# Expert weights fetched in longer pieces: gate and up chunks of 2 k-blocks x 1024 columns, down chunks with two neighbouring rows in each partition

## The chip, the cores and the metric

One of the eight cores of a Trainium2 chip runs the whole program. The metric is the device time of one execution in microseconds. Before the change it is 1585.43 us, the median of 3 runs (1585.12 to 1586.38).

## What is computed

The reference is two stacks of two layers each on 256 tokens of width 1024, all in float32. Only the last layer's feed-forward part, a mixture of eight experts, is touched by the change (hidden width 3584, two experts for each token):

```python
def swiglu(h, wg, wu, wd):
    return (jax.nn.silu(h @ wg) * (h @ wu)) @ wd

def moe_swiglu(h, w_router, wg, wu, wd):
    ...
    logits = (xt @ w_router).astype(jnp.float32)
    top_v, top_i = lax.top_k(logits, TOP_K)
    gates = jax.nn.softmax(top_v, axis=-1)
    gate = jnp.sum(jax.nn.one_hot(top_i, N_EXPERTS, dtype=jnp.float32) * gates[..., None], axis=1)
    y = jnp.zeros_like(xt)
    for e in range(N_EXPERTS):
        y = y + gate[:, e:e + 1].astype(xt.dtype) * swiglu(xt, wg[e], wu[e], wd[e])
```

Before it come a mixer layer pair (attention, convolution, gating), a second mixer with pooling and dilated attention, a dense swiglu of hidden width 2816 and a second such mixer; after it a final rmsnorm. Each expert's three matrices are 1024 x 3584, 1024 x 3584 and 3584 x 1024 floats.

## The kernel before

**Chunks.** Every large weight goes through one ring. SP (`sync_program`, for the experts `sp_chunk_moe`, L708 to L714) issues a DMA of one 1 MiB chunk into one of `RAW = 6` buffers `raw`, once DVE has finished with the chunk that lay there (`lo_ready`). ACT copies the chunk to `whi`, rounded to the shorter type fp32r (`act_hi_moe`, L993, two instructions of 128x1024, `hi_ready`). DVE subtracts that from the raw chunk and writes the rest to `wlo` (`dve_lo_moe`, L1374, two of 128x1024, `lo_ready`). `whi` and `wlo` have `SPLIT = 3` buffers; PE frees one when it has used it (`split_used`), so ACT starts the rounding of step i + 3 when PE ends step i.

**Jobs.** The experts' tokens are gathered into jobs: a heavy job takes 128 rows of one expert, a light job 64 rows. A pair is one heavy and one light job, and here four pairs cover the eight experts. A job is 42 chunks: 28 for gate and up and 14 for down, a pair 84 steps, all pairs 336. For each 128-row block of weights a heavy step multiplies three times (low part of x by high weights, high by low, high by high: L2595 to L2597), twelve matmuls of 512 columns in all; in a light step high and low part of x lie side by side in the 128 rows, so it multiplies twice (L2610, L2611), eight matmuls, and the two halves of the rows are added later by `fold`.

**Gate and up.** `job_chunks` cuts a job's hidden width into `BLOCKS = 7` blocks p of 512 columns. A block has two gate chunks and then two up chunks, each 4 k-blocks x 512 columns (`KC = 4`, `NC = 512`). Gate is summed in PSUM bank 0 of the job's two (`acc[:, job, 0]`), up in bank 1. After the last gate chunk of a heavy block ACT writes silu of the bank to `act_h` (L1294), after the last up chunk DVE multiplies bank 1 into it (L2046), two steps later PE transposes it (L2694, 4 matmuls), ACT rounds the result to `ahi2` (L1298) and DVE takes the rest to `alo2` (L2055). For a light block ACT copies the gate bank to `gate_l` (L1305) and the up bank to `value_l` (L1317), PE folds each (L2648, 8 matmuls), ACT applies silu (L1311), DVE multiplies (L2061), and ACT and DVE split the product into `alT` (L1321, L2066).

**Down.** The 28 row blocks of 128 hidden rows come as 14 chunks of 2 row blocks x 1024 columns; the row block k is rows 128k to 128k + 127, row 128k + p in partition p. Both banks of the job gather the 1024 output columns. They are read (`y_read`, L1278; `y_lo`, L2036) and scattered back into x (L2570, L2571, and `scattered`, L2025).

**Order.** `FIRST_ORDER` and `PAIR_ORDER` list which job each of a pair's 84 steps serves. The first pair leads with 12 heavy chunks (`LEAD = 12`), since the light job's expert is known only then; five of its chunks (steps 6 to 10) are loaded ahead into tiles that are still empty (`AHEAD`). From then on heavy and light alternate, and so they do in the other pairs, but for the first and last few steps. `plan_of` puts the silu, transpose, fold and split of a block a fixed number of steps behind its last chunk. Within one step i each engine has a fixed order: ACT first rounds chunk i + 3 (for which it waits until PE has ended step i) and then does silus and copies of step i; DVE first multiplies a heavy block that ended with step i, and then splits chunk i + 3. PE waits in `heavy_waits` and `light_waits` before the first chunk of a block, until the bank it is going to fill has been read: since a block's gate and up have a bank each, the reader has two further chunks of that job to do it in.

```python
up = [Chunk(which, p * NC, NC, k0, KC, p, k0 == 0, k0 + KC == KT)
      for p in range(BLOCKS) for which in "gu" for k0 in range(0, KT, KC)]
elif chunk.first and p:
    pe.wait_ge(hg_silu if chunk.which == "g" else h_act, done + p)
```

Of the kernel before, what the change touches and what calls it, by code (L numbers as in the profile page):

```python
# [25 lines left out]
PART = 128  # L26
# [165 lines left out]
LAST = BLOCKS - 1  # L192
# [9 lines left out]
def job_chunks():  # L202

    up = [Chunk(which, p * NC, NC, k0, KC, p, k0 == 0, k0 + KC == KT)
          for p in range(BLOCKS) for which in "gu" for k0 in range(0, KT, KC)]
    kt = D_FFE // PART
    return up, [Chunk("d", 0, WIDE, k0, WIDE_K, 0, k0 == 0, k0 + WIDE_K == kt) for k0 in range(0, kt, WIDE_K)]

# [124 lines left out]
def build(nc, A):  # L333

    ctx = ExitStack()
    with ctx:
# [12 lines left out]
        xhi = sb("xhi", [PART, KT, S], F32R)  # L349
        xlo = sb("xlo", [PART, KT, S], F32R)  # L350
# [42 lines left out]
        act_h = sb("act_h", [PART, NC], stack=moe)  # L393
# [41 lines left out]
        sb("below_alo2", [PART, NC + below], stack=ahead)  # L435
# [5 lines left out]
        big, big2 = (gate_l[:, 128 * i:128 * i + 128].rearrange("p (t n) -> p t n", t=TILES) for i in range(2))  # L441
# [90 lines left out]
        aT_ready = sem("aT_ready")  # L532
        hg_silu = sem("hg_silu")
# [70 lines left out]
        def h_tp(p):  # L604

            return tp[:, p % 2, :]

        def l_tp(p):

            n = NC // PART * LIGHT  # L610
            return tp[:, 2 + p % 2, 0:n], tp[:, 2 + p % 2, n:2 * n]

        def l_parts(p):

            parts = alT[:, p * NC:(p + 1) * NC].rearrange("p (k two n) -> p k two n", two=2, n=LIGHT)
# [100 lines left out]
        def sp_ahead(sp, src, e, chunk):  # L716
# [5 lines left out]
            sp.dma_start(raw_ahead[e][:, 0:chunk.k, 0:chunk.n],  # L722
# [49 lines left out]
        def sync_program(sp):  # L772
# [22 lines left out]
            def expert(e):  # L795
                return {"g": rows(wg, e), "u": rows(wu, e), "d": rows(wd, e)}
# [246 lines left out]
        def scalar_program(act):  # L1043
# [236 lines left out]
            def pair(j, plan):  # L1280
                done = BLOCKS * j
                for i in range(PER):
# [6 lines left out]
                    if i in plan.gate[HEAVY_JOB]:  # L1289
                        p = plan.gate[HEAVY_JOB][i]  # L1290
# [1499 lines left out]
```

## Time and profile before

| | us |
|---|---|
| median of 3 runs | 1585.43 (1585.12 to 1586.38) |
| profiled execution, its own time | 1585.69 |
| its span (first to last instruction) | 1583.9 |
| PE busy (mean granted clock 0.984) | 1523.3 (96%) |
| DVE busy | 1285.2 (81%) |
| ACT busy | 1104.4 (70%) |
| DMA queue q1, share of 16 engines | 78.5% |
| read from HBM | 460.29 MB, 291 GB/s over the span |

The experts' part begins at about 669 us and takes the rest of the span. In the page's row of 40 slices each slice is 39.6 us; a digit is a busy share in tenths. Busy shares of PE rest on modelled ends of matmuls, so that a PE with small gaps reads as full. A DMA share over 1 means that packets' times on one DMA engine overlap.

### The profile page before, as it was taken

To read this page: it belongs to the slowest core of one execution; us is meant where nothing else is said; L and a number is where in the kernel's file an instruction comes from. 1 tells how busy PE (TensorE), PEld (TensorE's weight loads), DVE (VectorE), ACT (ScalarE), POOL (GpSimd) and SP (SyncE) were. 2 spreads that over 40 slices of the span, in tenths; PEclk is the share of its full clock that TensorE was granted. 3 is DMA by queue.
4 is the path that set the end of the run, shared out by engine and by line. 5 is a ranking of instruction groups with operands and counts; after the bars stand their busy time and mean duration, and the time that the engine had idled before them with its cause. 6 is when DMAs were issued, how large, how long until landed. Compare 5 with 4: busy or idle time off the path is not lost.

```text
span 1583.9 us, 20830 instructions
## 1 busy us (share of the span) xinstructions
PE 1523.3 (96%) x7379; PEld 1259.0 (79%) x7379; DVE 1285.2 (81%) x1555; ACT 1104.4 (70%) x1475; POOL 118.7 (7%) x242
## 2 busy tenths in 40 slices
PE   6999999999999999699999999999999999999995
PEld 5788788888888888588887788788787887787784
DVE  5686585566545556689999999999999999999998
ACT  3664564645434364278888888888888888788886
POOL 3433431101000010100000000000000000000000
PEclk9999999999999999699999999999999999999998
DMA  9545444535545554369999999999999999999995
GB/s 330 202 156 173 156 158 135 182 116 186 173 146 198 193 179 160 136 230 372 391 397 406 393 385 387 387 406 407 385 386 387 391 408 400 384 387 386 399 407 224
DMA packets 203364, 462.70 MB, mean 292 GB/s; under 512 B 7934, under 2 KB 12428, under 8 KB 203132
## 3 DMA queue, kind: packets, MB, share of 16 engines
q1 hardware_dynamic: 200304, 453.80, 78.5%
q0 software_dynamic: 1904, 5.38, 1.3%
q10 hardware_dynamic: 1052, 2.19, 0.4%
q8 instruction: 59, 0.97, 0.3%
q14 instruction: 45, 0.37, 0.1%
HBM read 460.29 MB, written 1.05 MB: 291 GB/s over the span
## 4 chain that ended last, share of the span: by engine, by line
PE 67%; DMA 13%; DVE 12%; issue 3%; ACT 2%; DVEq 2%; SPq 0%; ACTq 0%
PE ps L2138 8%; PE ps L2139 8%; PE ps L2140 8%; DVE wlo_sb L1378 8%; DMA raw_sb<-moe_wu 7%; PE ps L2595 6%; PE ps L2597 6%; PE ps L2596 6%; PE ps L2610 5%; PE ps L2611 5%; DMA raw_sb<-moe_wg 2%; DMA raw_sb<-moe_wd 2%; ACT whi_sb L998 2%; DMA raw_sb<-w_in 2%; PE ps L2556 2%
## 5 line engine op out<-in xcount | busy, mean ns | idle before, releaser
L1378 DVE TENSOR_TENSOR wlo_sb<-raw_sb,whi_sb 128x1024 fp32r<-128x1024 f32 x662 | 772.6, 1219 | 44.8 <-ACT whi_sb L998 42.1
L998 ACT ACTIVATE whi_sb<-raw_sb 128x1024 fp32r<-128x1024 f32 x662 | 661.3, 1053 | 137.9 <-PE ps L2597 69.5
L1370 DVE TENSOR_TENSOR wlo_sb<-raw_sb,whi_sb 128x1024 fp32r<-128x1024 f32 (+2 forms) x198 | 230.1, 1203 | 146.1 <-ACT whi_sb L990 145.1
L990 ACT ACTIVATE whi_sb<-raw_sb 128x1024 fp32r<-128x1024 f32 (+2 forms) x198 | 192.3, 1023 | 163.3 <-PE ps L2140 131.8
L2138 PE MATMUL ps<-whi_sb,xlo_sb 128*128 128x512 f32 (+2 forms) x544 | 212.8, 391 | 4.4 <-DVE xlo_sb L1417 4.2
L2139 PE MATMUL ps<-wlo_sb,xhi_sb 128*128 128x512 f32 (+2 forms) x544 | 208.5, 383 | 0.0
L2140 PE MATMUL ps<-whi_sb,xhi_sb 128*128 128x512 f32 (+2 forms) x544 | 208.4, 383 | 0.0
L2595 PE MATMUL ps<-whi_sb,xlo_sb 128*128 128x512 f32 x448 | 181.5, 405 | 5.7 <-DVE wlo_sb L1378 4.4
L2610 PE MATMUL ps<-whi_sb,xhi_sb 128*128 128x512 f32 x448 | 177.8, 397 | 2.2 <-DVE wlo_sb L1378 2.1
L2597 PE MATMUL ps<-whi_sb,xhi_sb 128*128 128x512 f32 x448 | 175.4, 391 | 0.0
L2611 PE MATMUL ps<-wlo_sb,xhi_sb 128*128 128x512 f32 x448 | 175.0, 391 | 0.0
L2596 PE MATMUL ps<-wlo_sb,xhi_sb 128*128 128x512 f32 x448 | 174.4, 389 | 0.0
L2138 PEld LDWEIGHTS ps<-whi_sb,xlo_sb 128*128 128x128 f32 x544 | 103.2, 190 | 26.0 <-DVE wlo_sb L1370 4.6
L2140 PEld LDWEIGHTS ps<-whi_sb,xhi_sb 128*128 128x128 f32 x544 | 103.0, 189 | 19.4
L2139 PEld LDWEIGHTS ps<-wlo_sb,xhi_sb 128*128 128x128 f32 x544 | 103.2, 190 | 18.8 <-issue 0.5
L2595 PEld LDWEIGHTS ps<-whi_sb,xlo_sb 128*128 128x128 f32 x448 | 84.2, 188 | 30.6 <-issue 8.9
L2610 PEld LDWEIGHTS ps<-whi_sb,xhi_sb 128*128 128x128 f32 x448 | 84.1, 188 | 21.3 <-DVE wlo_sb L1378 3.6
L2597 PEld LDWEIGHTS ps<-whi_sb,xhi_sb 128*128 128x128 f32 x448 | 84.1, 188 | 18.9
L2611 PEld LDWEIGHTS ps<-wlo_sb,xhi_sb 128*128 128x128 f32 x448 | 84.2, 188 | 16.6
L2596 PEld LDWEIGHTS ps<-wlo_sb,xhi_sb 128*128 128x128 f32 x448 | 84.4, 188 | 15.8
L2610 PE MATMUL ps<-whi_sb,alT_sb 128*128 128x512 f32 x224 | 90.2, 403 | 4.0 <-DVE wlo_sb L1378 2.8
L2595 PE MATMUL ps<-whi_sb,alo_sb 128*128 128x512 f32 x224 | 90.4, 404 | 1.0 <-DVE wlo_sb L1378 0.9
(394 smaller groups left out, 2129.2 us busy)
## 6 DMA issues: line engine op xcount, KB each, us to landing
raw_sb<-moe_wg SPq DMA_DIRECT2D x113, 1024.0 KB, 11.3
raw_sb<-moe_wd SPq DMA_DIRECT2D x112, 1024.0 KB, 10.9
raw_sb<-moe_wu SPq DMA_DIRECT2D x109, 1024.0 KB, 11.9
raw_sb<-w_in SPq DMA_DIRECT2D x40, 1024.0 KB, 5.2
raw_sb<-w_out SPq DMA_DIRECT2D x16, 1024.0 KB, 5.0
raw_sb<-ffn_wg SPq DMA_DIRECT2D x10, 1024.0 KB, 5.1
raw_sb<-ffn_wu SPq DMA_DIRECT2D x10, 1024.0 KB, 5.1
raw_sb<-ffn_wd SPq DMA_DIRECT2D x10, 1024.0 KB, 5.1
```

Source lines behind the costliest of these rows:

```text
L990: nc.scalar.activation(whi[i % SPLIT][:, c:c + k // 2, 0:n], raw[i % RAW][:, c:c + k // 2, 0:n], ACT.Copy).then_inc(hi_ready, 1)
L998: nc.scalar.activation(whi[i % SPLIT][:, c:c + KC // 2, :], moe_raw(i, l)[:, c:c + KC // 2, :], ACT.Copy).then_inc(hi_ready, 1)
L1370: op = V.tensor_tensor(wlo[i % SPLIT][:, c:c + k // 2, 0:n], raw[i % RAW][:, c:c + k // 2, 0:n], whi[i % SPLIT][:, c:c + k // 2, 0:n], ALU ...
L1378: op = V.tensor_tensor(wlo[i % SPLIT][:, c:c + KC // 2, :], moe_raw(i, l)[:, c:c + KC // 2, :], whi[i % SPLIT][:, c:c + KC // 2, :], ALU.s ...
L2138: mm(out, lo, whi[i % SPLIT][:, c, 0:chunk.n], start=first, stop=False)
L2139: mm(out, hi, wlo[i % SPLIT][:, c, 0:chunk.n], start=False, stop=False)
L2140: op = mm(out, hi, whi[i % SPLIT][:, c, 0:chunk.n], start=False, stop=last)
L2595: mm(o, lo, whi[i % SPLIT][:, w, :], start=first, stop=False)
L2596: mm(o, hi, wlo[i % SPLIT][:, w, :], start=False, stop=False)
L2597: op = mm(o, hi, whi[i % SPLIT][:, w, :], start=False, stop=last)
L2610: mm(o, both, whi[i % SPLIT][:, w, :], start=first, stop=False)
L2611: op = mm(o, both, wlo[i % SPLIT][:, w, :], start=False, stop=last)
```

## The change

Gate and up of an expert are cut into three groups q of 1024 columns, each with four chunks of 2 k-blocks x 1024 columns for gate and then four for up, and a last group of 512 columns with chunks as before. A row piece of such a chunk is 1024 columns, 4 KB, where it was 512 columns, 2 KB. For down, the rows of a chunk are dealt out as `(p c)` where they were `(c p)`: partition p takes rows 2p and 2p + 1, which lie behind each other, 8 KB in one piece. So that the hidden values meet the right rows, the readers of the PSUM banks deal them out in the same way: `in_blocks` reads a bank with even columns and odd columns apart (every second float), and writes them as blocks of 128.

A wide group's gate now fills both banks of its job, and so does its up. PE goes through a wide chunk one bank after the other, signals at the end of the first bank's last matmul (`h_half_ps`), and waits before each bank's first matmul of up until silu has read that bank (`heavy_bank_free`), and before the light job's up until its copy is done. `act_h` holds 1024 columns, and lies in the half of `xlo` that no one uses. The light job's gate and up share one row buffer `row_l`. Transposes, folds, roundings and products of a wide group are done at once: 4 times in a job where there were 7.

```diff
 def job_chunks():
 
-    up = [Chunk(which, p * NC, NC, k0, KC, p, k0 == 0, k0 + KC == KT)
-          for p in range(BLOCKS) for which in "gu" for k0 in range(0, KT, KC)]
+    up = [Chunk(which, q * WIDE, WIDE, k0, WIDE_K, q, k0 == 0, k0 + WIDE_K == KT)
+          for q in range(WIDE_BLOCKS) for which in "gu" for k0 in range(0, KT, WIDE_K)]
+    up += [Chunk(which, WIDE_BLOCKS * WIDE, NC, k0, KC, WIDE_BLOCKS, k0 == 0, k0 + KC == KT)
+           for which in "gu" for k0 in range(0, KT, KC)]
...
+        def act_h_of(p):
+
+            return act_h[:, 4 * (p % 2):4 * (p % 2) + 4, :].rearrange("p (s two) n -> p s two n", two=2)
+
+        def in_blocks(bank):
+
+            return bank.rearrange("p (s n two) -> p s two n", n=PART, two=2)
...
-        def rows(w, l):
+        def rows(w, l, neighbours=False):
+
+            order = "(p c)" if neighbours else "(c p)"
...
-                return {"g": rows(wg, e), "u": rows(wu, e), "d": rows(wd, e)}
+                return {"g": rows(wg, e), "u": rows(wu, e), "d": rows(wd, e, neighbours=True)}
...
                     if i in plan.gate[HEAVY_JOB]:
-                        p = plan.gate[HEAVY_JOB][i]
+                        q = plan.gate[HEAVY_JOB][i]
+                        if not first(j) or q:
+                            act.wait_ge(hT_ps, done + q)
+                        for p in blocks_of(q):
+                            if p % 2 == 0 and q < WIDE_BLOCKS:
+                                act.wait_ge(h_half_ps, 2 * WIDE_BLOCKS * j + 2 * q + 1)
+                            else:
+                                act.wait_ge(split_used, number(AT_MOE, i + 1, PER, j))
+                            nc.scalar.activation(act_h_of(p), in_blocks(h_bank(p, "g")), ACT.Silu).then_inc(hg_silu, 1)
...
-                        V.tensor_tensor(act_h[:, :], acc[:, HEAVY_JOB, 1, :], act_h[:, :], ALU.mult).then_inc(h_act, 1)
+                        for p in blocks_of(q):
+                            if p % 2 == 0 and q < WIDE_BLOCKS:
+                                dve.wait_ge(h_half_ps, 2 * WIDE_BLOCKS * j + 2 * q + 2)
+                            else:
+                                dve.wait_ge(split_used, number(AT_MOE, i + 1, PER, j))
+                            dve.wait_ge(hg_silu, BLOCKS * j + p + 1)
+                            V.tensor_tensor(act_h_of(p), in_blocks(h_bank(p, "u")), act_h_of(p), ALU.mult).then_inc(h_act, 1)
...
+            def heavy_bank_free(chunk, j, h):
+
+                q = chunk.block
+                if chunk.which == "u" and chunk.n == WIDE:
+                    pe.wait_ge(hg_silu, BLOCKS * j + 2 * q + h + 1)
+                elif q:
+                    pe.wait_ge(h_act, BLOCKS * j + 2 * (q - 1) + bank_of(chunk, h) + 1)
+                elif h == 0 and not first(j):
+                    pe.wait_ge(yg_lo, 4 * j)
...
+                elif chunk.first and chunk.which == "u" and chunk.n == WIDE:
+                    pe.wait_ge(lg_copied, done + q + 1)
+                elif chunk.first and q:
+                    pe.wait_ge(lu_copied, done + q)
```

**The queue of SP**, the last up and first down chunks of the first pair's heavy job, before:

```order
L713 DMA raw_sb<-moe_wg 128x4x512
L713 DMA raw_sb<-moe_wu 128x4x512 [waits lo_ready] x4
L713 DMA raw_sb<-moe_wd 128x2x1024 [waits lo_ready]
L713 ISA [waits lo_ready]
L713 DMA raw_sb<-moe_wg 128x4x512
L713 DMA raw_sb<-moe_wd 128x2x1024 [waits lo_ready]
```

and after the change (heavy and light chunks take turns in both; ISA works out an expert's address):

```order
L757 DMA raw_sb<-moe_wu 128x2x1024 [waits lo_ready]
L757 DMA raw_sb<-moe_wu 128x4x512 [waits lo_ready]
L757 DMA raw_sb<-moe_wu 128x2x1024 [waits lo_ready]
L757 DMA raw_sb<-moe_wd 128x2048 [waits lo_ready]
L757 ISA [waits lo_ready]
L757 DMA raw_sb<-moe_wg 128x2x1024
L757 DMA raw_sb<-moe_wd 128x2048 [waits lo_ready]
```

Gate and up are moved as 2 pieces of 1024 floats for each partition where they were 4 of 512, except in the last group; a down chunk's 2 pieces of 1024 have become one of 2048.

**ACT at the head of the first pair**, before (xhi and xlo are the gathered tokens, whi the rounded weights, the ahead tiles the chunks loaded ahead):

```order
L998 ACTIVATE whi_sb<-raw_sb 128x1024 x4
L1294 ACT_TABLE_LOAD
L1294 ACTIVATE act_h_sb<-ps 128x512
L998 ACTIVATE whi_sb<-raw_sb 128x1024 x2
L998 ACTIVATE whi_sb<-ahead_in_alo_sb 128x1024 x2
L998 ACTIVATE whi_sb<-ahead_in_alT_sb 128x1024 x2
L998 ACTIVATE whi_sb<-ahead_in_y_sb 128x1024 x2
L1294 ACTIVATE act_h_sb<-ps 128x512
L1298 ACTIVATE ahi_sb<-ps 128x512
```

and after the change:

```order
L1044 ACTIVATE whi_sb<-raw_sb 128x1024 x6
L1044 ACTIVATE whi_sb<-ahead_in_alo_sb 128x1024 x2
L1344 ACT_TABLE_LOAD
L1344 ACTIVATE xlo_plain_sb<-ps 128x4x128 x2
L1044 ACTIVATE whi_sb<-ahead_in_alT_sb 128x1024 x2
L1044 ACTIVATE whi_sb<-ahead_in_y_sb 128x1024 x2
```

The silu of a group stands behind the rounding of the chunk loaded into `ahead_in_alo`, which is that of step 6, and both its halves follow each other (`xlo_plain` is the tile of `act_h`).

**PE at the first up chunk of the first pair's heavy job**, before (the end of the last gate step, and the start of the first up step):

```order
L2595 MATMUL ps<-whi_sb,xlo_sb 128x512
L2596 MATMUL ps<-wlo_sb,xhi_sb 128x512
L2597 MATMUL ps<-whi_sb,xhi_sb 128x512
L2595 MATMUL ps<-whi_sb,xlo_sb 128x512 [waits lo_ready]
L2596 MATMUL ps<-wlo_sb,xhi_sb 128x512
```

and after the change:

```order
L2663 MATMUL ps<-whi_sb,xhi_sb 128x512
L2661 MATMUL ps<-whi_sb,xlo_sb 128x512 [waits hg_silu,lo_ready]
L2662 MATMUL ps<-wlo_sb,xhi_sb 128x512
L2663 MATMUL ps<-whi_sb,xhi_sb 128x512
L2661 MATMUL ps<-whi_sb,xlo_sb 128x512
L2662 MATMUL ps<-wlo_sb,xhi_sb 128x512
L2663 MATMUL ps<-whi_sb,xhi_sb 128x512
L2661 MATMUL ps<-whi_sb,xlo_sb 128x512 [waits hg_silu]
L2662 MATMUL ps<-wlo_sb,xhi_sb 128x512
```

The first up step has a wait for silu ahead of each of its two banks, where it had none.

## Rows read from the trace of the kernel before

**Rows 1.** The page's slices of 39.6 us: DMA share in tenths, rate
```profile
DMA  9545444535545554369999999999999999999995
GB/s 330 202 156 173 156 158 135 182 116 186 173 146 198 193 179 160 136 230 372 391 397 406 393 385 387 387 406 407 385 386 387 391 408 400 384 387 386 399 407 224
```

**Rows 2.** Windows: us, PE, PEld, DVE, ACT, POOL busy, PEclk, DMA share, GB/s
```profile
690.00:710.00 20.00, 20.00 (x106) 17.06 (x105) 16.82 (x21) 14.52 (x21) 0.00 (x0) 1.00 0.49 156
...
720.00:740.00 20.00, 20.00 (x100) 16.79 (x99) 19.27 (x20) 17.11 (x22) 0.00 (x0) 1.00 1.03 373
1200.00:1220.00 20.00, 19.61 (x96) 15.88 (x95) 18.86 (x20) 17.57 (x22) 0.00 (x0) 1.00 1.05 386
1280.00:1300.00 20.00, 20.00 (x104) 16.79 (x103) 17.00 (x18) 17.25 (x27) 0.00 (x0) 1.00 1.03 409
```

**Rows 3.** The DMA's packets in 1200 to 1220 us (gate, up), then 1290 to 1310 (down)
```profile
DMA packets 3877, 7.72 MB, mean 386 GB/s; under 512 B 116, under 2 KB 116, under 8 KB 3875
...
DMA packets 2121, 8.17 MB, mean 408 GB/s; under 512 B 127, under 2 KB 127, under 8 KB 2121
```

**Rows 4.** ACT in order of time: start us, us, line; one such row in each pair
```profile
914.86 0.58 ACT L1327 ACTIVATE backT_sb<-ps 128x512 fp32r<-128x512 f32 x1
...
1363.58 0.58 ACT L1327 ACTIVATE backT_sb<-ps 128x512 fp32r<-128x512 f32 x1
```

**Rows 5.** SP's waits in 914.9 to 1363.6 us: total us, times, longest
```profile
SPq L713 <- DVE wlo_sb L1378: 340.2, 169, 5.5
```

**Rows 6.** Windows, one pair: columns as in group 2
```profile
1139.30:1363.60 224.30, 219.86 (x1033) 178.95 (x1031) 215.02 (x209) 189.31 (x228) 0.00 (x0) 1.00 1.04 393
```

**Rows 7.** Groups of DVE and ACT in that pair: busy us, mean ns, idle before
```profile
L1378 DVE TENSOR_TENSOR wlo_sb<-raw_sb,whi_sb 128x1024 fp32r<-128x1024 f32 x169 | 197.3, 1219 | 9.2 <-ACT whi_sb L998 8.6 <-issue 0.2
L2046 DVE TENSOR_TENSOR act_h_sb<-ps,act_h_sb 128x512 f32<-128x512 f32 x7 | 4.8, 683 | 0.0
...
L998 ACT ACTIVATE whi_sb<-raw_sb 128x1024 fp32r<-128x1024 f32 x168 | 167.8, 1052 | 35.0 <-PE ps L2597 15.5 <-DMA raw_sb<-moe_wg 7.1 <-DMA raw_sb<-moe_wu 4.7
```

**Rows 8.** PE in order of time: 23 matmuls in a row, and a fold
```profile
1179.84 0.39 PE L2595 MATMUL ps<-whi_sb,xlo_sb 128*128 128x512 f32 x1
...
1184.83 0.39 PE L2597 MATMUL ps<-whi_sb,xhi_sb 128*128 128x512 f32 x1
...
1187.11 0.39 PE L2611 MATMUL ps<-wlo_sb,xhi_sb 128*128 128x512 f32 x1
1187.34 1.00 PE L2648 MATMUL ps<-con_moe_sb,value_l_sb 128*128 128x64 f32 x8
1188.15 0.48 PE L2595 MATMUL ps<-whi_sb,xlo_sb 128*128 128x512 f32 x1
1188.46 0.39 PE L2596 MATMUL ps<-wlo_sb,xhi_sb 128*128 128x512 f32 x1
```

**Rows 9.** ACT in order of time at the head of the first pair
```profile
674.69 2.01 ACT L998 ACTIVATE whi_sb<-raw_sb 128x1024 fp32r<-128x1024 f32 x2 [0.71 <-PE ps L2597]
676.72 1.28 ACT L1294 ACT_TABLE_LOAD   x1
678.01 0.60 ACT L1294 ACTIVATE act_h_sb<-ps 128x512 f32<-128x512 f32 x1
678.51 2.00 ACT L998 ACTIVATE whi_sb<-raw_sb 128x1024 fp32r<-128x1024 f32 x2
680.40 2.00 ACT L998 ACTIVATE whi_sb<-ahead_in_alo_sb 128x1024 fp32r<-128x1024 f32 x2
```

**Rows 10.** PE in order of time there: a gather, a transpose, the next step
```profile
685.31 0.64 PE L2556 MATMUL ps<-pick_sb,xnhi_sb 128*128 128x192 f32 x4
...
686.24 0.60 PE L2694 MATMUL ps<-con_sb,act_h_sb 128*128 128x128 f32 x4
686.60 0.47 PE L2595 MATMUL ps<-whi_sb,xlo_sb 128*128 128x512 f32 x1
```

**Rows 11.** SP in order of time: its last DMA issues
```profile
1553.50 1.49 SPq L713 DMA_DIRECT2D raw_sb<-moe_wg  x3
```

More of the change, by code:

```diff
@@ L2606, in light_step @@
                     first, last = chunk.first and c == 0, chunk.last and c == chunk.k - 1
-                    for h in range(chunk.n // NC):
-                        o = out[:, h if chunk.which == "d" else "gu".index(chunk.which), :]
-                        w = c * (chunk.n // NC) + h
-                        mm(o, both, whi[i % SPLIT][:, w, :], start=first, stop=False)
-                        op = mm(o, both, wlo[i % SPLIT][:, w, :], start=False, stop=last)
-                op.then_inc(split_used, 1)
+                    o = acc[:, LIGHT_JOB, bank_of(chunk, h), :]
@@ new lines, in light_step @@
+                    w = c * (chunk.n // NC) + h
+                    mm(o, both, whi[i % SPLIT][:, w, :], start=first, stop=False)
+                    op = mm(o, both, wlo[i % SPLIT][:, w, :], start=False, stop=last)
+                op.then_inc(split_used, 1)
+            def heavy_bank_free(chunk, j, h):
[6 more added lines that the diff above has]
+                    pe.wait_ge(yg_lo, 4 * j)
@@ L2645, in fold @@
-            def fold(out, src):
-                for a in range(NC // PART):
-                    op = mm(out[:, a * LIGHT:(a + 1) * LIGHT], src[:, a * PART:(a + 1) * PART], C("fold"), start=True,
+                        pe.wait_ge(lg_copied, done + GROUPS)
+                        pe.wait_ge(lu_copied, done + GROUPS)
+                    if chunk.k0 * PART % WIDE == 0:
+                        pe.wait_ge(l_lo, done + chunk.k0 * PART // WIDE + 1)
+                elif chunk.first and chunk.which == "u" and chunk.n == WIDE:
+                    pe.wait_ge(lg_copied, done + q + 1)
+                elif chunk.first and q:
+                    pe.wait_ge(lu_copied, done + q)
+                elif chunk.first and first(j):
+                    xg_read(1, ROUNDS)
+                elif chunk.first:
+                    pe.wait_ge(yg_lo, 4 * j + 2)
@@ L2649, in fold @@
+            def fold(q, which):
+                out = l_tp(q, which)
+                for a in range(NC * len(blocks_of(q)) // PART):
+                    at = a % (NC // PART) * LIGHT
+                    op = mm(out[:, a // (NC // PART), at:at + LIGHT], row_l[:, a * PART:(a + 1) * PART], C("fold"), start=True,
                             stop=True)
```

238 lines of the change are left out of this document (124 added, 114 removed).

## The prediction

> **What bounds the kernel now.** I read the page's slices first, then windows, the DMA's packets, the waits, and the groups of one pair. The slices split the program in two [rows 1]: until about 690 us the DMA carries 116 to 230 GB/s (330 in the first slice), afterwards its share is 9 in every slice, at 372 to 407 GB/s. That second part is the experts' weights, and the only part the change touches.
>
> Within it the rate has two levels, and each holds steadily: 386 GB/s while gate and up arrive, 409 while down arrives [rows 2]. The packets say what differs. In 20 us of gate and up 3877 less 116 small ones carry 7.72 MB, 2 KB each; in 20 us of down 2121 less 127 carry 8.17 MB, 4 KB each [rows 3]. A chunk of 1,048,576 bytes thus takes 2.713 us in 512 pieces of 2 KB, and 2.567 us in 256 of 4 KB. The DMA sets the pace: 56 x 2.713 + 28 x 2.567 = 223.8 us for a pair, and the pair's mark on ACT recurs every (1363.58 - 914.86) / 2 = 224.4 us [rows 4]. SP waits for DVE ahead of each issue [rows 5], 340.2 / 169 = 2.0 us; with six buffers that fixes how far ahead the queue is filled, and does not show an idle DMA.
>
> But three others are close behind. In a pair of 224.3 us DVE is busy 215.0 [rows 6], with 9.2 us idle, 8.6 of it for a rounding by ACT [rows 7]. PE's busy time says little, so I count: 23 matmuls start within 1184.83 - 1179.84 = 4.99 us, 0.227 us apart, and a fold holds up the next step by 1188.15 - 1187.34 = 0.81 us, with 0.08 us more on its first matmul [rows 8]. A pair is 840 x 0.227 = 190.5, 14 folds x 0.89 = 12.5, 7 transposes x 0.44 = 3.1, 4 gathers x 0.93 = 3.7 [rows 10], and 16 scatter matmuls x 0.227 = 3.6: 213.4 us. ACT, 189.3 [rows 6], has room.
>
> **What the pieces are worth.** From the two levels, 16 packets fewer on each of the 16 DMA engines save 2.713 - 2.567 = 0.146 us, 9.1 ns a packet. Of a pair's 56 gate and up chunks 48 become 4 KB pieces: 48 x 0.146 = 7.0 us. An 8 KB piece has no row; the bounds are 2.713 us for a chunk (no better than 2 KB) and, by the same price per packet, 8 x 9.1 ns less than 4 KB: 2.494 us. A loss can't be excluded, but the two levels are the nearest rows and I take 2.494, so 28 x 0.073 = 2.0 us. The DMA's own time for a pair falls from 223.8 to 214.7.
>
> The Trainium skill gives a rule against any such gain (DMA: Bandwidth & Descriptors, "Where 436 GB/s comes from"): for transfers between HBM and SBUF the HBM's share of some 358 GB/s binds. By it the pieces would be worth nothing. The trace does not agree, since down runs at 409.
>
> **What the others then allow.** DVE's 215.0 loses the fixed part of 9 instructions of 21 (turn, light product and light split: 4 for 7 each), about 0.07 us each: 214.4 us. PE loses the pauses around 6 folds and 3 transposes, 0.5 us: 212.9 us. So DMA, DVE and PE would stand within 2 us, and what decides is new waits.
>
> **The new waits of PE.** Before, a block's up went into its own bank. Now up of a wide group goes into the banks gate has filled, and PE must wait for their reader. Four places, three times in a pair, counted from the moment PE ends the step that closes a bank:
> - Heavy gate to up. ACT first rounds the next chunk, 2.0 us, and then writes silu, some 0.6 with 0.1 of overlap: 2.5 us [rows 9]. PE has one light step meanwhile, 8 x 0.227 = 1.8. It waits 0.7. The second bank's silu comes 0.5 us later, while PE needs 1.4 for the first.
> - Light gate to up. A copy of 1024 columns, priced as a rounding at 1.05 [rows 7], after the same 2.0: some 2.95 us against a heavy step of 2.7. 0.25.
> - Heavy up to the next gate. DVE's product, 0.68 for one instruction [rows 7], has to be done behind a split that PE needs anyway. 0.6.
> - Light up to the next gate, as the second. 0.25.
>
> Together 3 x 1.8 = 5.4 us for a pair. Where PE is idle anyway they cost nothing (the end is 214.7, DMA's time), where it is not they all count (212.9 + 5.4 = 218.3). I take **217.5**, near the upper end, since PE has under 2 us left to hide them in. Behind a PE that waits stands ACT, which rounds only when PE has ended a step, and then DVE; three buffers take up single waits of under a us, not a lasting lag.
>
> **The head of the first pair** has 12 heavy steps in a row, no light step in between, and PE is what limits there: DMA's share is 0.49 in 690 to 710 us [rows 2]. So its waits count in full. At step 4 PE waits for a rounding, the table load that has moved behind it, and silu: 674.69 to 678.61 in the row before, 3.9 us [rows 9]. At step 8 it waits for DVE's product, about 0.2. At step 12 for rounding and silu, 2.5, less a gather of 0.93 that stands between [rows 10]: 1.6. Sum **5.7 us**. The bounds are 0, if the queue makes it up, and 7.
>
> **The sum.** The DMA is saturated from 720 us [rows 2] to the last issue at 1553.5 [rows 11], 833 us or 3.7 pairs. 3.7 x (224.3 - 217.5) = 25.2 saved, 5.7 given back: 19.5 us. The profiled execution's own time is 1585.7, with 1.8 us outside its span, and lies 0.3 above the median. 1585.7 - 19.5 = **1566**. The tail behind the last chunk stays.
>
> **The strided reads** I cost at nothing. Silu, product and copies now take every second float of a PSUM bank. No row shows that; a doubled time per element is the upper bound. 512 columns more cost DVE 1.219 - 0.683 = 0.54 us, and ACT about 1.05 - 0.58 = 0.47 [rows 7, 9]. The nearest rows, dense reads of the same banks, speak for the lower end. The Trainium skill speaks for the upper (SBUF — State Buffer, "Door 1: The DMA port swizzle"): PSUM lines hold two floats, and non-contiguous patterns slow matmuls significantly. No run here shows it yet; its mechanism is the second rival.
>
> **Rivals.**
> 1. *The covers hold.* PE's waits fall into idle time and the DMA stays the bound: 3.7 x (224.3 - 214.7) = 35.5, and some half of the head's loss is made up: 1553. For it: ACT now waits 7.1 us for gate chunks alone to land [rows 7], so today's lags are absorbed. Against: PE and DVE would have to run with no idle time. Chance 0.18.
> 2. *PE's new waits become the bound and exceed the gain: slower.* The strided reads at their upper bound lengthen a group's four waits by 0.47, 0.95, 0.54 and 0.95: 8.7 us a pair. PE's pair is then 227.0, 2.7 more than now; 3.7 x 2.7 + 7.2 in the head gives 1603. It decides from the point where the new waits pass 224.3 - 5.7 / 3.7 - 212.9 = 9.9 us a pair, 3.3 for a group instead of my 1.8. For it: every wait lies on the engine with least room, and ACT starts each only after a rounding. Against: nothing shows dearer reads. Chance 0.13.
> 3. *The rate isn't the piece's.* Down differs from gate and up in more than its piece: its rows lie behind each other in HBM, those of gate and up 14,336 bytes apart. If that made the 386, or if bytes bound as in the rule above, gate and up gain nothing. With down's 2.0 a pair: 1585.7 - 7.4 + 5.7 = 1584; without it 1591. Against: both levels are steady, and 9.1 ns for a packet brings the rate for bytes alone to 1,048,576 / (2.567 - 16 x 0.0091) = 433 GB/s, a plausible limit above both. Chance 0.11.
> 4. *The change doesn't do what it says*, as far as 8 KB goes: the hardware could cut pieces. SP's order shows 2048 floats in one, so only the packets can tell. It costs the DMA 2.0 us a pair, which a pair of 217.5 hides; it is inside the forecast.
>
> **How the numbers follow.** Forecast 0.58, rivals 0.18, 0.13, 0.11. The forecast's own range runs from 1555 (3.7 x 8.3 = 30.7 saved in pairs of 216, nothing lost at the head) to 1573 (3.7 x 6.0 = 22.2 saved in pairs of 218.3, 7 lost at the head, 2 more for pieces that gain less). For 8 in 10 the range takes in the first rival's centre and the better half of the third: 1552 to 1587. A measurement of this kernel can tell 0.2%, 3.2 us. Faster by more: 0.56 + 0.18 + 0.02 = 0.76. Within it: 0.01 + 0.03 + 0.05 = 0.09. Slower: 0.01 + 0.10 + 0.04 = 0.15.
>
> **What the profile after would show.** Windows of gate and up at 400 GB/s or more if the DMA is still the bound; if not, its share under 1.0. Packets of 4 KB and 8 KB. The mark of a pair every 217.5 us. PE waiting for ACT's silu and for its copies of the light job, 0.25 to 0.7 us each, and at the first pair's fifth step 3.9 us. Silu at some 580 ns for 512 columns and DVE's product at 683, if strides cost nothing. The forecast is wrong if those are near a us, if gate and up stay at 386 with a share over 1, or if a pair takes 223 us or more.

## The result, and the profile after

| | before | changed |
|---|---|---|
| median, us | 1585.33 (1585.12 to 1586.38, 4 runs) | 1609.68 (1609.08 to 1615.66, 4 runs) |
| ratio, 95% interval | | 1.0161 [1.0136, 1.0185]: 1.6% slower |
| span of the profiled execution | 1583.9 | 1613.8 |
| a pair (ACT's mark, third to fourth) | 224.4 | 227.6 |
| DVE idle for ACT's rounding in a pair | 8.6 | 13.5 |

The forecast was 1566 us, in a range from 1552 to 1587. The change costs 24 us. The profiled execution of the changed kernel took 1615.66 us, 6.0 over the median; it ran at a lower granted clock before its first mark (0.61 in 660 to 680 us, against 0.84 in `e3_gateup_only` below), so I read the head of the first pair from that kernel and this profile for the rest.

The page of the changed kernel: slices of 40.3 us (DMA share in tenths, rate), packets, the main queue, and the chain that ended last.

```profile
DMA  9546543626455646249999999999999999999995
GB/s 329 201 145 181 166 150 129 198 79 209 157 184 182 211 161 225 75 178 357 374 397 400 372 381 383 384 384 396 386 395 377 393 375 409 378 393 382 383 391 220
DMA packets 139107, 462.69 MB, mean 287 GB/s; under 512 B 7934, under 2 KB 12428, under 8 KB 124540
...
PE 74%; DVE 14%; ACT 5%; issue 3%; DVEq 2%; DMA 2%; SPq 0%; ACTq 0%
```

The rates no longer stand on two levels as in [rows 1]. They wander from 372 to 409 GB/s, below what the pieces allow, and the DMA makes up 2% of the chain, where it was 13% before. ACT in order of time, its mark in each pair (start us, us, line):

```profile
936.71 0.60 ACT L1378 ACTIVATE backT_sb<-ps 128x512 fp32r<-128x512 f32 x1
...
1164.52 0.60 ACT L1378 ACTIVATE backT_sb<-ps 128x512 fp32r<-128x512 f32 x1
...
1392.07 0.60 ACT L1378 ACTIVATE backT_sb<-ps 128x512 fp32r<-128x512 f32 x1
```

227.8 and 227.6 us from mark to mark, against 224.4 in [rows 4]. Windows of the changed kernel, columns as in [rows 2]: a whole pair, and 20 us of down.

```profile
936.70:1164.50 227.80, 221.32 (x1034) 178.86 (x1033) 213.64 (x200) 187.09 (x213) 0.00 (x0) 1.00 1.00 387
...
1340.00:1360.00 20.00, 20.00 (x88) 16.05 (x87) 19.79 (x18) 16.88 (x18) 0.00 (x0) 1.00 1.01 420
```

DVE works 1.4 us less than in [rows 6], and the pair is 3.4 us longer: 14.2 us of it DVE stands idle. Down now reaches 420 GB/s, where it had 409. What was waited for in that pair (engine, line, releaser: total us, times, longest):

```profile
ACT whi_sb L1044 <- PE ps L2663: 34.3, 33, 2.5
DVE wlo_sb L1429 <- ACT whi_sb L1044: 13.5, 13, 2.2
...
PE ps L2661 <- ACT xlo_plain_sb L1344: 1.8, 2, 1.0
...
PEld ps L2676 <- ACT row_l_sb L1355: 1.6, 3, 0.6
...
PE ps L2661 <- DVE xlo_plain_sb L2101: 0.9, 3, 0.3
PE ps L2676 <- ACT row_l_sb L1355: 0.4, 2, 0.2
```

ACT's 14.6 us of waits for chunks to land (7.1 and 4.7 in [rows 7], 2.8 for down) have gone from the list. In their place it waits for PE, 34.3 us where it was 15.5; most of that rise is not yet a loss, since in `e1_pieces_only`, 38 us faster, the same entry is 27.9. PE's own new waits are small: the three lines of PE for silu and product (1.8, 0.9) and for the copy (0.4) make 3.1 us (PEld is the weight load, which overlaps PE), where 5.4 were forecast. DVE waits 13.5 us where it was 8.6. How a delay of PE reaches DVE is seen in order of time at one group (PE, ACT and DVE; in brackets the idle time before and who ended it):

```profile
1208.21 1.06 ACT L1344 ACTIVATE xlo_plain_sb<-ps 128x512 f32<-128x512 f32 x2
1208.92 0.47 PE L2661 MATMUL ps<-whi_sb,xlo_sb 128*128 128x512 f32 x1 [0.74 <-ACT xlo_plain_sb L1344]
...
1211.05 1.02 ACT L1355 ACTIVATE row_l_sb<-ps 128x1024 f32<-128x1024 f32 x1
...
1212.13 0.50 PE L2676 MATMUL ps<-whi_sb,xhi_sb 128*128 128x512 f32 x1 [0.22 <-ACT row_l_sb L1355]
...
1214.08 1.89 PE L2722 MATMUL ps<-con_moe_sb,row_l_sb 128*128 128x64 f32 x16
1214.34 2.01 ACT L1044 ACTIVATE whi_sb<-raw_sb 128x1024 fp32r<-128x1024 f32 x2 [0.33 <-PE ps L2677]
1215.79 0.48 PE L2661 MATMUL ps<-whi_sb,xlo_sb 128*128 128x512 f32 x1
...
1218.88 2.01 ACT L1044 ACTIVATE whi_sb<-raw_sb 128x1024 fp32r<-128x1024 f32 x2 [2.54 <-PE ps L2663]
```

PE waits 0.74 for silu and 0.22 for the copy, then folds 16 matmuls in a row (1214.08 to 1215.79), and only then begins the heavy step that frees a buffer. ACT can round again at 1218.88, after 2.54 us idle, and DVE's next split comes at 1219.98 after 2.18 idle. From one rounding to the next are 4.54 us (1214.34 to 1218.88), DVE's split takes 2.36, and the difference is its 2.18 idle. Gaps of 2.19 and 2.18 us stand at 992.42 and 1036.00 too. In this stretch the fold on PE moves the moment at which a buffer comes free, and DVE gets it with no discount.

### The profile page after: what moved, and what is told of

It is laid out like the page before. It is cut to its first block, busy times and chain, and to the rows that moved or that the text cites. A ratio compares the mean times of both kernels' runs of the same rounds, so it can differ in the third digit from the quotient of the medians.

```text
span 1613.8 us, 20607 instructions
## 1 busy us (share of the span) xinstructions
PE 1538.0 (95%) x7379; PEld 1264.1 (78%) x7379; DVE 1279.4 (79%) x1519; ACT 1095.8 (68%) x1415; POOL 118.3 (7%) x242
## 3 DMA queue, kind: packets, MB, share of 16 engines
q10 hardware_dynamic: 1052, 2.19, 0.4%
HBM read 460.29 MB, written 1.05 MB: 286 GB/s over the span
## 4 chain that ended last, share of the span: by engine, by line
PE 74%; DVE 14%; ACT 5%; issue 3%; DVEq 2%; DMA 2%; SPq 0%; ACTq 0%
DVE wlo_sb L1429 9%; PE ps L2193 8%; PE ps L2194 8%; PE ps L2195 8%; PE ps L2661 8%; PE ps L2663 7%; PE ps L2662 7%; PE ps L2676 6%; PE ps L2677 5%; ACT whi_sb L1044 3%; PE ps L2722 3%; DMA raw_sb<-w_in 2%; PE ps L2611 1%; PE ps L2771 1%; DVEq L2081 1%
```

## The experiments

Three theories and a rival were tested. Theory 1: the pieces pay as priced, and what costs is PE's new waits and lumps. The rival: strided reads of PSUM. Theory 2: DVE's 2.2 us gaps come from the lump of the doubled folds (the expectations of e5 and e6 still call it theory 1, and theory 2 in that of e1 is the forecast's third rival). Theory 3: the loop PE, ACT, DVE, PE over three split buffers has no room, so that a delay anywhere on PE reaches DVE in full.

### e1_pieces_only

SP's fetches alone are changed, to the pieces of the changed kernel.

```diff
+            chunk = as_wide(chunk)
...
+            return chunk._replace(n0=chunk.block // 2 * WIDE, n=WIDE, k0=chunk.k0 + 2 * (chunk.block % 2), k=WIDE_K)
...
-                return {"g": rows(wg, e), "u": rows(wu, e), "d": rows(wd, e)}
+                return {"g": rows(wg, e), "u": rows(wu, e), "d": rows(wd, e, neighbours=True)}
```

> The kernel before, with only SP's fetches changed: gate and up chunks of blocks 0 to 5 are fetched as 2 k-blocks x 1024 columns, down chunks with two neighbouring rows in each partition; what is multiplied, all waits and all engines stay as before. The values in the buffers are dealt out wrongly, so the experts' sums are not the reference's. Theory 1 (the pieces are worth what the two levels of the rate say, and the loss comes from new waits and larger lumps of work on PE, which make DVE idle in the loop PE, ACT, DVE): a pair at 216 to 219 us instead of 224.3, 1560 to 1568 us in all, and the engines no longer wait for the DMA. Theory 2 (the rate of gate and up is not set by the piece): a pair at 222 to 224, 1578 to 1586, gate and up still at 386 GB/s.

Measured: 1571.35 us (1571.21 to 1575.69), ratio 0.9919 [0.9902, 0.9935], 14 us faster than before. Its windows for one pair, and DVE's split in it (busy us, mean ns, idle before):

```profile
1133.10:1353.50 220.40, 218.04 (x1033) 179.50 (x1032) 213.56 (x209) 186.53 (x228) 0.00 (x0) 1.00 1.01 401
...
L1388 DVE TENSOR_TENSOR wlo_sb<-raw_sb,whi_sb 128x1024 fp32r<-128x1024 f32 x169 | 196.3, 1220 | 6.7 <-ACT whi_sb L1008 6.1 <-issue 0.2
```

The time lies 3 us above what was expected. The pieces are worth 3.9 us a pair, and no chunk is waited for any more. But the pair is 220.5 us, not the 216 to 219 expected: with the DMA out of the way DVE still idles 6.7 us, in lumps of up to 1.33 us around the end of up and 0.36 us once in a block. So the three engines' busy sums are not what a pair takes, even without a single new wait.

### e2_down_only and e3_gateup_only

One half of the change each. Down alone is the kernel before, with neighbouring rows and the readers that deal banks out in even and odd columns; gate and up alone is the changed kernel with dense readers:

```diff
-            return bank.rearrange("p (s n two) -> p s two n", n=PART, two=2)
+            return bank.rearrange("p (s n) -> p s n", n=PART)
...
-                return {"g": rows(wg, e), "u": rows(wu, e), "d": rows(wd, e, neighbours=True)}
+                return {"g": rows(wg, e), "u": rows(wu, e), "d": rows(wd, e)}
```

> The kernel before with the down part of the change alone: 8 KB pieces, and strided reads of the PSUM banks in silu, product and copies, nothing else. Theory 1: 28 x 0.073 = 2.0 us a pair less for the DMA, of which DVE's and PE's lags may eat half: 1578 to 1583. Rival (strided reads cost): silu, product and copies above 580 and 683 ns, and no gain or a loss, 1585 or more.

> The changed kernel with down as before: 4 KB pieces with rows dealt as before, and dense reads of the banks. Theory 1: down's piece and the strides have no part in the loss, a pair stays at 227 to 228 us and the time within 3 us of the changed kernel, 1607 to 1613. Rival (strides or 8 KB pieces made the loss): 1600 or less.

Measured: down alone 1578.29 us, 0.9955 [0.9938, 0.9971]; gate and up alone 1609.85, 1.0155 [1.0138, 1.0172]. Both are as expected. The whole loss lies in gate and up: with down's pieces and strided reads the changed kernel takes 1609.68, without both 1609.85. That the two don't cancel is seen in e2, where the strided silu takes 578 ns for 577 before and the product 685 for 683. So strided reads have no part in the loss, and 8 KB pieces are worth nothing to a kernel that the DMA doesn't bound. The marks of e3 (719.19, 928.52, 1156.38, 1384.55) against those of e1 (709.97, 912.57, 1133.06, 1353.51) say where the 36.8 us between their spans (1606.3 and 1569.5) arise: 9.2 ahead of the first mark, 6.7 up to the second, 7.4 and 7.7 in the next two, 5.8 behind the last mark.

### e4_silu_ahead

The changed kernel, with the silu of a group's first bank ahead of the rounding instead of behind it.

```diff
+                    if early:
+                        act.wait_ge(h_half_ps, 2 * WIDE_BLOCKS * j + 2 * q + 1)
+                        nc.scalar.activation(act_h_of(2 * q), in_blocks(h_bank(2 * q, "g")), ACT.Silu).then_inc(hg_silu, 1)
                     act_hi_moe(act, i + SPLIT, j)
```

> The changed kernel with one move on ACT: the silu of a wide group's first bank stands ahead of the rounding of chunk i + 3 instead of behind it. Theory 1: PE's 0.7 us waits at each heavy gate to up go, and at the head some 2 to 3 us of the 4; the folds' lumps stay, and the rounding comes 0.5 us later, which may make DVE idle in its place. 3 x 0.5 us a pair and 3 at the head: 1600 to 1606. If the waits for silu were the whole of the loss: 1590 or less. If they do nothing: 1609.

Measured: 1599.32 us, 1.0089 [1.0073, 1.0106]; 10.4 under the changed kernel, a little better than expected. 3.5 us of it are won ahead of the first mark (715.72 for 719.19), and a pair is 226.5. PE's waits for silu, 1.8 us a pair, are gone from its list, and a pair gets 1.2 back: the waits for silu are part of the loss, not most of it.

### e5_folds_split and e6_all_spread

A wide group's fold of 16 matmuls becomes two of 8 a few steps apart. The second kernel adds e4's edit, transposes in two halves with the first a step earlier, and silu's table load ahead of the experts.

```diff
-                for a in range(NC * len(blocks_of(q)) // PART):
+                for a in range(NC // PART * part, NC // PART * (part + 1)):
...
+                    if i in plan.fold_g2:
+                        fold(plan.fold_g2[i], "g", 1).then_inc(lgT_ps, 1)
```

> The changed kernel, whose folds of a wide light group (16 matmuls in one go, some 1.7 us, behind one step) are done as two lots of 8 behind two steps of that job; silu, product and split of the group come two steps later. Same work, same waits for silu and copies. Theory 1 (lumps of PE work in the three-step loop make DVE idle; the trace of the changed kernel has idle times of 1.7 to 2.2 us on DVE behind each gate fold, three in a pair): they fall below 1 us, a pair goes from 227.6 to 222 to 225, 1593 to 1602. Rival (the waits alone make them): stays within 3 us of the changed kernel, 1607 to 1612.

> The changed kernel with all of it: folds in two lots, first bank's silu ahead of the rounding, first bank's four transposes one step earlier than the second's, and the table for silu loaded by an idle ACT before the first pair. Theory 1: DVE's idle time in a pair falls to the 5 to 6 us that are left without wide groups' waits, a pair at 219 to 222, the head's delay below 2 us: 1570 to 1582. Rival (the pace of gate and up is limited by the DMA or by DVE otherwise): above 1590.

Both miss. Measured: 1612.95 us, 1.0161 [1.0144, 1.0178], and 1601.70, 1.0093 [1.0076, 1.011]. DVE in order of time in e5, at one group:

```profile
1201.33 2.36 DVE L1435 TENSOR_TENSOR wlo_sb<-raw_sb,whi_sb 128x1024 fp32r<-128x1024 f32 x2 [0.81 <-ACT whi_sb L1050]
1217.64 4.63 DVE L1435 TENSOR_TENSOR wlo_sb<-raw_sb,whi_sb 128x1024 fp32r<-128x1024 f32 x4 [1.30 <-ACT whi_sb L1050]
1223.12 4.74 DVE L1435 TENSOR_TENSOR wlo_sb<-raw_sb,whi_sb 128x1024 fp32r<-128x1024 f32 x4 [0.84 <-ACT whi_sb L1050]
```

The gaps of 2.2 us are gone, and others of 1.30 and 0.84 stand in their place: 2.95 us for a group, where the changed kernel has 0.50 + 2.19 + 0.81 = 3.50 at 985.53 to 1013.92. A pair takes 226.9 us, 0.8 less than in the changed kernel, and not the 222 to 225 expected. Theory 2 falls, the lump isn't what makes the pair long; nor can it be the sum of the folds, since e1 has the same 112 fold matmuls in its pair of 220.5. What makes these gaps stays open. The total of e5 is a poorer test than its pair: its silu and product of the light job come two steps later, and in the first pair (214.6 us from mark to mark, 209.3 in e3) PE waits 2.44 us at 862.43 for that product. e6 is no better than e4 alone.

### e7_waits_added and e12_waits_inner

e1 with PE's new waits and nothing else of the change: at up of blocks 0, 2 and 4 in the first, of 2 and 4 in the second.

```diff
+                elif chunk.first and chunk.which == "u" and p in (2, 4):
+                    pe.wait_ge(hg_silu, done + p + 1)
+                    if p:
+                        pe.wait_ge(h_act, done + p)
```

> The kernel with the pieces alone (wrong values, work and lots as in the kernel before), to which only the changed kernel's waits of PE are added: before the first up chunk of blocks 0, 2 and 4 PE waits for silu (heavy) or the copy (light) of the same block's gate. The banks don't need it. Theory 1 by the prediction's price: 3 x (0.7 + 0.25) = 2.9 us a pair if nothing overlaps, and 3 to 6 us at the head: 1571 + 11 + 5 = 1587. If PE's waits fall into idle time: 1571 to 1577, and then the lots of work make the rest. If they alone made the loss: 1600 or more.

> e7_waits_added, but with PE's waits for silu, product and copies only ahead of the up chunks of blocks 2 and 4, where heavy and light chunks take turns, and not of block 0, where three chunks of a job stand in a row and the waits were 3 us long. Values are dealt out wrongly, as in e1_pieces_only. Theory 3 (waits of PE reach DVE in full): two groups at 1.9 to 2.4 us each, pair 224.3 to 225.3; with 3.7 pairs and some 1 to 4 us at the first pair's head, 1586 to 1592 us. Rival (single waits under a microsecond are taken up by the three buffers): pair 220.5 to 222, 1572 to 1579.

Measured: e7 1608.71 us, 1.0134 [1.0117, 1.0151], 37 over e1; e12 1582.34, 0.9985 [0.9976, 0.9995], 11 over e1. By its expectation e7's time would make the waits the whole loss. It says less than that: in the narrow order three chunks of one job stand in a row at block 0, and PE waited 2.6 and 2.7 us there, which the changed kernel doesn't. What it does give is a price: PE's waits of 4.3 and 2.7, 7.0 us in a pair, made the pair 7.3 to 8.7 us longer than e1's. e12 leaves that place out. What was waited for in one of its pairs:

```profile
DVE wlo_sb L1388 <- ACT whi_sb L1008: 8.0, 14, 1.3
...
PEld ps L2605 <- ACT act_h_sb L1304: 2.5, 2, 1.2
...
PE ps L2605 <- ACT act_h_sb L1304: 1.7, 2, 0.8
```

Its pair (mark 1139.68 to 1362.37) takes 222.7 us, 2.2 over e1's: two waits of together 1.7 us on PE cost the pair 2.2. That is below the 224.3 expected and above the rival's 222; per group it is 1.1 us, not 1.9 to 2.4. A wait of PE does reach the pair in full, 2.2 for 1.7 here and 7.3 to 8.7 for 7.0 in e7. By the same price the 3.1 us that PE waits in a pair of the changed kernel make some 3 to 4 (an estimate) of the 7.2 us by which its pair exceeds e1's.

### e8_half_release

The changed kernel, and a split buffer is handed back in halves: PE signals when it has used a half, and ACT rounds into that half while PE works on the other.

```diff
-            act.wait_ge(split_used, number(AT_MOE, i - SPLIT + 1, PER, l))
-            for c in range(0, KC, KC // 2):
+            for n, piece in enumerate(pieces(chunk_at(plan, i))):
+                if n:
+                    act.wait_ge(split_used, number(AT_MOE, i - SPLIT + 1, PER, l))
+                else:
+                    act.wait_ge(half_used, number(0, i - SPLIT + 1, PER, l))
```

> The changed kernel; only the buffers of the split weights are handed back in halves: PE signals when it has used the first half of a step's weights, and ACT may then round the first half of the chunk three steps on, instead of at the end of the step. Pieces are cut the way a wide chunk is multiplied, one bank after the other. Theory 3 (no engine and not the DMA bounds the changed kernel, but the loop PE ends a step, ACT rounds, DVE splits, PE starts three steps on: with three buffers it has no room, so each wait or lump of PE reaches DVE in full): the loop gains about 0.9 to 1.3 us of room, DVE's idle time in a pair falls from 14 to 4 to 8 us, 1580 to 1595. Rival (the room is not what is missing, the waits themselves are): stays within 4 us of the changed kernel.

Measured: 1577.40 us (1577.03 to 1578.14), 0.9953 [0.9937, 0.997]. No wait is removed from the program, no engine does less, and 32.3 us have gone, more than expected (1580 to 1595). In its pair from 1137.4 to 1358.2, first the windows, then the waits:

```profile
1137.40:1358.20 220.80, 218.58 (x1033) 179.72 (x1033) 214.00 (x200) 190.17 (x214) 0.00 (x0) 1.00 1.02 400
```

```profile
ACT whi_sb L1063 <- PE ps L2705: 22.5, 42, 2.1
DVE wlo_sb L1448 <- ACT whi_sb L1063: 5.3, 10, 0.9
...
PE ps L2725 <- ACT row_l_sb L1374: 0.4, 2, 0.2
```

DVE waits 5.3 us for the rounding where it was 13.5, with the longest 0.9 for 2.2. This is what theory 3 said. But the experiment does two things: ACT's rounding now begins before PE has ended its step, so silu comes sooner too, and of PE's 3.1 us of waits for silu, product and copy only the 0.4 for the copy are left. How much of the 7.2 us a pair is room in the loop and how much the shorter waits, e8 alone doesn't tell; e4, where the waits for silu are gone and the buffers are whole, got 1.2.

### e11_pieces_release

The control for e8: the same halves in e1, where no new wait stands.

```diff
-            act.wait_ge(split_used, number(AT_MOE, i - SPLIT + 1, PER, l))
+            act.wait_ge(half_used, number(0, i - SPLIT + 1, PER, l))
             for c in range(0, KC, KC // 2):
+                if c:
+                    act.wait_ge(split_used, number(AT_MOE, i - SPLIT + 1, PER, l))
```

> The kernel before with its fetches in 4 KB and 8 KB pieces (as in e1_pieces_only: values are dealt out wrongly, the work per engine is that of the kernel before) and with the split buffers handed back in halves, as in e8_half_release, but with none of the changed kernel's new waits. It says how much of the 32 us that halves gave the changed kernel belongs to the new waits. Theory 3 (the loop of three buffers has no room, and a new wait of PE reaches DVE in full; halves make the room): without the waits there are only some 6 us of idle DVE in a pair of 220.5 to win, and the DMA's own 214.7 and DVE's 213.6 are near: pair 217.5 to 219.5, 1560 to 1567 us, a gain of 4 to 11 us over e1's 1571.4, a third of the 32 or less. Rival: halves shorten every step, waits or not, and the gain is nearly the same here: down to the floor of 214.7 for a pair, some 1550 us. Second rival: without the waits halves give nothing, pair 220 to 221, 1570 to 1573.

Measured: 1563.06 us (1562.93 to 1564.88), 0.9864 [0.9849, 0.9879], a pair of 218.1 (two pairs from 908.94 to 1345.22), as theory 3 expected, and 3.4 us over the DMA's 214.7. With it a table can be made, time and pair in us:

| | whole buffers | halves | gain |
|---|---|---|---|
| pieces alone (e1, e11) | 1571.35, 220.5 | 1563.06, 218.1 | 8.3 |
| with the new waits and wide groups (changed, e8) | 1609.68, 227.7 | 1577.40, 220.5 | 32.3 |
| the wide groups cost | 38.3 | 14.3 | 24.0 |

A quarter of what halves gave is there without the new structure. The other 24 us belong to the waits and wide groups: delays that halves take up, or, as PE's waits for silu, don't let arise.

### e10_down_halves

Halves, and a start of PE on the first half, in e2, where gate and up still come in 2 KB pieces.

> The kernel before with the down part of the change (8 KB pieces), and both signals in halves, gate and up still in 2 KB pieces. Here the DMA is the bound, 56 x 2.713 + 28 x 2.494 = 221.8 us a pair, of which the down part alone already has 222.8. Theory 3: more room in the loop gains at most 1 us a pair, 1574 to 1578. If it gained more, the 2 KB pieces would not be a bound.

Measured: 1575.72 us, 0.9943 [0.9926, 0.9959]; a pair of 222.6 (two from 908.53 to 1353.73), where e2 has 222.8 (912.32 to 1357.88). More room in the loop gives a pair nothing while the DMA bounds it, with gate and up at 386 GB/s as in [rows 2]. It is the longer pieces that make the room worth having: with them halves give 2.4 us a pair (e1 to e11), without them 0.2 (e2 to e10).

### e9_halves_all

e8, and PE starts on a step when its first split half is there; with e4's silu, the earlier transposes and the early table load of e6.

```diff
+                if not START or (first(j) and i < SPLIT):
+                    pe.wait_ge(lo_ready, whole)
+                    return None
+                pe.wait_ge(lo_half, number(0, i - SPLIT + 1, PER, j))
+                return pieces(chunk)[1][0], whole
```

> The same handing back in halves, and PE also starts a step when the first half of its weights is split; with it the first bank's silu ahead of the rounding, the first bank's transposes a step earlier, and the silu table loaded before the first pair. Theory 3: a pair at DVE's own 214 to 217 us, 1560 to 1572, below the kernel before and below the down part alone (1578). Rival (as above): 1590 or more.

Measured: **1565.65 us** (1565.36 to 1567.64), 0.9877 [0.986, 0.9893]. It is the fastest of the kernels that do the whole computation, 19.7 us under the kernel before (1585.33) and 44.0 under the changed one. Of the 11.8 us that it gains over e8 no run says how they divide among its four edits. A pair, and the 20 us of gate and up that stand in [rows 2]; under them the packets of those 20 us:

```profile
1129.90:1348.80 218.90, 217.94 (x1032) 179.44 (x1032) 213.29 (x200) 189.86 (x213) 0.00 (x0) 1.00 1.02 403
1200.00:1220.00 20.00, 19.95 (x96) 16.42 (x95) 19.96 (x20) 18.14 (x21) 0.00 (x0) 1.00 1.03 409
```

```profile
DMA packets 2114, 8.18 MB, mean 409 GB/s; under 512 B 122, under 2 KB 122, under 8 KB 2112
```

Gate and up in 4 KB pieces run at 409 GB/s once the engines keep up, exactly down's level in [rows 3], though their rows lie 14,336 bytes apart. Its head shows one gain: PE waits 0.35 us for the first silu, not 4.15.

## Why the prediction was wrong

- **The DMA's part held.** 2,121 and 3,877 packets [rows 3] gave 9.1 ns each, 2.567 us for a chunk in 4 KB and 2.494 in 8 KB. Those are 408 and 420.4 GB/s; e9 shows 409 in gate and up, the changed kernel 420 in a window that is mostly down. Ten us of down alone in e2, from 1260 to 1270 us, hold 515 packets of 8 KB besides the 64 small ones:

```profile
DMA packets 579, 4.22 MB, mean 422 GB/s; under 512 B 64, under 2 KB 64, under 8 KB 64
```

  Rival 3 (the rate isn't the piece's) and rival 4 (no 8 KB) fall. The rule of the Trainium skill that was weighed there (DMA: Bandwidth & Descriptors, "Where 436 GB/s comes from"), some 358 GB/s for HBM, would have made all pieces worthless; e1's 14 us and windows of 399 to 420 GB/s say otherwise.
- **Strided reads cost nothing**, as costed. The groups of the changed kernel in the pair from 936.7 us:

```profile
L2101 DVE TENSOR_TENSOR xlo_plain_sb<-ps,xlo_plain_sb 128x512 f32<-128x512 f32 x7 | 4.5, 686 | 0.0
L1344 ACT ACTIVATE xlo_plain_sb<-ps 128x512 f32<-128x512 f32 x8 | 4.4, 583 | 0.0
```

  The product took 683 ns before [rows 7]. The Trainium skill's caution on non-contiguous PSUM patterns (SBUF — State Buffer, "Door 1: The DMA port swizzle") speaks of matmuls, and reads by ACT and DVE don't show it. The second rival's mechanism was therefore wrong; that its sign came true and its 1603 lies near the 1609.7 is luck.
- **PE's waits were foreseen at the right places and too long in sum**: heavy gate to up 0.7 (0.74 and 1.0 measured), light 0.25 (0.22), heavy up to next gate 0.6 (0.3), head 3.9 (4.15). In a pair 5.4 us were forecast and 3.1 measured, so their lengths were not underrated; their price was.
- **"What the others then allow" failed, and by the largest amount.** It set DVE's 214.4 and PE's 212.9 us of work beside the DMA's 214.7 and took the largest as the length of a pair without new waits. e1 has no new wait and takes 220.5. The profile of before had a hint: 9.2 us of DVE's idle time, 8.6 of it for ACT [rows 7]. The forecast let it vanish with the faster DMA; 6.7 of it stayed. In the sum that is 220.5 - 214.7 = 5.8 us a pair, 3.7 x 5.8 = 21 us. Halves give e1 2.4 of the 5.8 back (e11); what holds the other 3.4 is open, and no kernel here reached 214.7.
- **"Where PE is idle anyway they cost nothing" and "three buffers take up single waits of under a us" failed too.** The forecast charged the new waits 217.5 - 214.7 = 2.8 us a pair. Measured are 227.7 - 220.5 = 7.2, for waits and all else that the wide groups bring: 4.4 a pair or 16 us too little. With this error alone the sum gives 1582, with the one above alone 1588, both about the 1585 of before; it takes the two together, and the head, to reach the loss. ACT rounds into a buffer only when PE has ended a whole step. Half a rounding (1.05 us) and a split (2.36) later the chunk is ready, while PE has two steps, 1.8 + 2.7 us, until it needs it: about one us of room (an estimate from those rows) for all that stands on ACT and DVE between. With DVE busy 97% of e1's pair, idle time it has once had is hardly made up. e8, with the reservation made there, shows that it is this circle, in which ACT waits for whole steps: the same work and 7.2 us a pair back. By the prices of e7 and e12 PE's waits are some 3 to 4 of the 7.2. The rest must come with the wide groups, whose side work on PE is the same in sum but comes in larger lots: folds of 16, two silus in a row, a copy of 1.02 us, two products in a row. How it divides among these stays open; cutting the folds alone (e5) gained 0.8.
- **The head** was to cost 5.7 us and cost 9.0: from the first expert step to the first mark e3 takes 719.19 - 667.95 = 51.24 us, e1 709.97 - 667.74 = 42.23. e1's PE waits for none of this. The first stall was sized rightly, 4.15 for 3.9; the other two are in e3:

```profile
698.49 0.47 PE L2661 MATMUL ps<-whi_sb,xlo_sb 128*128 128x512 f32 x1 [0.70 <-DVE xlo_plain_sb L2101]
...
714.18 0.47 PE L2661 MATMUL ps<-whi_sb,xlo_sb 128*128 128x512 f32 x1 [1.86 <-ACT xlo_plain_sb L1344]
```

  That is 0.70 for 0.2 and 1.86 for 1.6, in all 6.7 us. 1.4 us were left out right behind the first, where PE ran at little over half its pace (below). The last 0.9 I can't place.
- **The sum, mended.** e1's 1571.35, 3.7 pairs by 7.2 = 26.6, and 9.0 at the head make 1607; 1609.7 was measured. (These terms are measured, not forecast: they show where the time lies, not that it could be foreseen.) The first rival (the covers hold, 1553) had the same fault as the forecast, more so. The second put the point of decision at 9.9 us of waits a pair, and PE's rows show 3.1. The point is much lower: the pieces gave 3.9 us a pair, and whatever the wide groups cost above that is a loss.

## What to carry to other kernels

Busy sums are floors, not periods. Where three engines stand within 2% of each other and pass buffers round in a circle, work out how long the circle takes for one buffer, and compare that with the steps it has; if there is little slack, a wait put on one engine of it can count in full, even on one that looks idle: e12's 1.7 us made 2.2, e7's 7.0 made 7.3 to 8.7. Handing a buffer back in the pieces in which it is used is worth trying before one moves work about: here it gave 32 us with no instruction of compute less, and turned a change that lost 24 us into one that gains 8 (e8), and, with four further edits, 20 (e9).

## What the runs showed of the hardware

A stall of PE can cost more than its length. PE of e3_gateup_only in order of time, the fifth step of the first pair:

```profile
683.23 0.68 PE L2661 MATMUL ps<-whi_sb,xlo_sb 128*128 128x512 f32 x1 [4.15 <-ACT xlo_plain_sb L1344]
683.71 0.63 PE L2662 MATMUL ps<-wlo_sb,xhi_sb 128*128 128x512 f32 x1
684.14 0.63 PE L2663 MATMUL ps<-whi_sb,xhi_sb 128*128 128x512 f32 x1
...
686.70 0.42 PE L2663 MATMUL ps<-whi_sb,xhi_sb 128*128 128x512 f32 x1
686.96 0.40 PE L2661 MATMUL ps<-whi_sb,xlo_sb 128*128 128x512 f32 x1
687.20 0.40 PE L2662 MATMUL ps<-wlo_sb,xhi_sb 128*128 128x512 f32 x1
```

After 4.15 us idle the matmuls start 0.43 us apart, and from 686.96 on 0.23 as before. The granted clock is 0.53 in 683.2 to 685.0 us, the lower of its two levels (1.2 for 2.4 GHz), and 1.00 in 676 to 679, before the stall, and in 687 to 690. From 683.71 to 686.96 eight starts take 3.25 us for 8 x 0.227 = 1.82, so 1.4 us more. The granted clock in 680 to 700 us is 0.91 there, and 1.00 in the same stretch of the kernel before. In the changed kernel's own profile ten starts behind the same stall, from 688.30 to 692.56 us, take 4.26 us for 2.27, 2.0 more, at a granted clock of 0.50. In e8_half_release the stall is 3.15 us, and behind it the clock is 0.50 in 682 to 684 us. In e4_silu_ahead the same place has waits of 1.44 and 0.66 us on PE instead, and the granted clock is 1.00 in 680 to 700 us.

The rate of weights into SBUF went with the piece: 386 GB/s at 2 KB, 409 at 4 KB, and 418 to 424 at 8 KB in six stretches of 10 us of e2's down (1260 to 1320 us). At 4 KB it was the same whether the pieces lie behind each other in HBM (down before) or 14,336 bytes apart (gate and up in e9).
